# Attention of a two-block network: the order of its token tiles is reversed

## The chip, the cores and the metric

One NeuronCore of a Trainium2 chip runs the whole network as one program. The metric is the device time of one execution in microseconds (us). Engines are named as the profile names them: PE (TensorE), DVE (VectorE), ACT (ScalarE), POOL (GpSimd), SP (SyncE, which issues most DMAs).

## The reference, cut to what matters

The input is 512 tokens of width 1024, in float32. The first block has two layers; each is a feed-forward part, a hybrid mixer, and a second feed-forward part. The second block has two layers of another kind, which the change does not touch. In the mixer, one projection feeds three branches; only the attention branch and the projection matter here:

```python
proj = h @ w_in                                   # 512 x 1024 by 1024 x D_IN
# attention, 8 heads in 2 groups of 4, head width 64, blocks of 128 query tokens
p_s = masked_softmax(q @ k_sel.T + bias_s, dist_s >= 0)    # "selected": top_n covers all blocks
p_w = masked_softmax(q @ k_win.T + win_bias, causal mask)  # "window" of 512 = all tokens
o   = g0 * o_c + g1 * (p_s @ v_sel) + g2 * (p_w @ v_win)
```

With 512 tokens both attentions are causal attention over all earlier tokens: a query tile i (128 tokens) needs keys of tiles 0 to i, that is (i + 1) * 128 keys. The query tiles do not depend on each other. `masked_softmax` subtracts the row maximum, exponentiates and divides by the sum.

## The kernel before, in words

The program is a sequence of stages. A stage has one instruction stream for each engine, written out by hand, and ends with a barrier of all engines. Products of float32 values are made from a high part (`..._high`, rounded) and a low part (`..._low`, the rest), with three matmuls (`product`, lines 163 to 165). The high part is made by ACT (a CAST), the low part by DVE (`low_part`, line 170).

The change lies in `mixer1_attend`, the stage `attn_0` in the first layer and `attn_1` in the second. It does two things at once:

- **Attention.** `pairs` lists 16 steps p, each a query tile i and a head a of each group (so two heads). Every step has two half steps m = 2p + b: b = 0 for the selected keys, b = 1 for the window keys. For a half step, PE makes the scores (`scores(m)`, line 1430), DVE adds the bias and takes the row maximum (`biased(m)`, line 1576, and line 1580 for the shift), ACT exponentiates (`exps(m)`, line 1525), PE transposes the probabilities (`turn(m)`, line 1441), ACT and DVE copy the two groups out (`copy(m)`, lines 1533 and 1586), and PE multiplies with the values (`values(m)`, line 1455). After both half steps DVE combines (`combine(p)`, lines 1593 to 1606). The width of all this is `keys(m)` = (i + 1) * 128.
- **Dense pieces.** The part LATE of the projection (20 output tiles in 8 chunks of weights: 12 wide ones of 512 columns, 8 narrow ones of 256) is cut into pieces of 2 or 4 of the 8 contraction steps. `dense_plan` spreads these pieces, in a fixed order, over the 32 half steps, in proportion to `room` = 10.0 - 1.6 * (i + 1) of the half step. It counts 0.68 for a contraction step of a wide tile, 0.36 for a narrow one.

The PE order in one step p is: `scores(2p)`, `turn(2p-2)`, `dense(2p)`, `scores(2p+1)`, `values(2p-2)`, `turn(2p-1)`, `dense(2p+1)`, `values(2p-1)`. `scores(m)` waits until `biased(m-1)` is done, since all scores use the same two PSUM banks. A dense tile n waits until tile n-2, which used its bank, is evacuated.

In half step h, after their attention work, ACT and DVE evacuate the tiles that ended in half step h-1 and make the high and low parts of the next chunks of weights (`next_pieces`: four quarters for each of chunks 2 to 7). Chunk 0 is split at the head of the stage, one contraction step after another. Chunk 1 is split whole: `round_high(1)` stands in ACT's stream behind `exps(0)`, and `round_low(1)` in DVE's between `biased(0)` and `biased(1)`. DVE also has one convolution for each of the six `raw` tiles (`convolve`, lines 1623 to 1628), two half steps after the tile's last piece, and `positions` (line 1635). SP loads a chunk once the chunk two before it is split, and the next stage's first weights once the last chunk is split.

Of the kernel before, what the change touches and what calls it, by code (L numbers as in the profile page):

```python
# [24 lines left out]
TT = T // P  # L25
# [11 lines left out]
HPG = HEADS // GROUPS  # L37
# [1203 lines left out]
def mixer1_part(w_in, order):  # L1241
    chunks = mixer1_chunks(w_in)
    return [chunks[c] for c in order]
# [130 lines left out]
def mixer1_attend(nc, M, A, I, l, mine, ahead):  # L1374
# [2 lines left out]


    chunks, tiles = mixer1_part(I.w_in[l], LATE), mixer1_tiles(A, LATE)
    pairs = [(i, a) for i in range(TT) for a in range(HPG)]  # L1380
    N = len(pairs)
    plan = dense_plan(tiles, [10.0 - 1.6 * (i + 1) for i, _ in pairs for b in range(2)])
    half_of = {n: half for half, here in enumerate(plan) for n, _, end in here if end == DT}
# [902 lines left out]
def mixer1(nc, M, I, l, mine, ahead):  # L2286
    with ExitStack() as outer:
# [6 lines left out]
        with ExitStack() as memory:  # L2294
            sb = tensors(nc, memory, f"a{l}_")
            M.bias = sb("bias", HEADS, T)
            A.bias_all = M.bias
            A.qT = sb("qT", HPG, T)
            A.ksT, A.kwT = sb("ksT", T), sb("kwT", T)
            A.vs, A.vw = sb("vs", TT, KV), sb("vw", TT, KV)  # L2300
            A.gates = sb("gates", TT, HEADS * N_BRANCH)
            A.silz, A.dt, A.a = sb("silz", TT, D_SSM), sb("dt", TT, SH), sb("a", TT, SH)
            A.dt_e, A.dt_u, A.dt_r, A.dt_ln = (sb(f"dt_{x}", TT, SH) for x in "eurl")
            A.d_skip, A.norm_g = sb("d_skip", SG), sb("norm_g", SG)
            A.uv = sb("uv", TT, 2 * D_GMLP)
            A.raw = sb("raw", XT, T + SCONV - 1)
            A.blk = A.mix_local[:].rearrange("p i n -> p (i n)").rearrange("p (j m g n) -> p j m g n", j=2, g=GROUPS, m=PAIRS)
            A.zT = A.silz[:].rearrange("p i n -> p (i n)").rearrange("p (c t) -> p c t", t=T)
            A.gates_dtT = A.mix_local[0:HEADS * N_BRANCH + SH, 0, :]
            A.vT = A.mix[:, 0:2, :]  # L2310
            A.cmp_b = sb("cmp_b", CMP_HID)
            A.cmp_pos, A.cmp_w2, A.ws = sb("cmp_pos", 2, PAIRS), sb("cmp_w2", 2, 2, GROUPS, HD), sb("ws", GG, P)
            A.conv_w, A.conv_b, A.ws_b = sb("conv_w", SCONV, XT), sb("conv_b", XT), sb("ws_b", GG)
            A.ln_g, A.ln_b = sb("ln_g", D_GMLP), sb("ln_b", D_GMLP)
            A.dt_bias, A.a_log, A.a_neg = sb("dt_bias", SH), sb("a_log", SH), sb("a_neg", SH)
            rest_ahead = compression_ahead(nc, M, f"rest_{l}", I.cmp_w1[l])
            late_ahead = chunks_ahead(nc, M, f"attn_{l}", mixer1_part(I.w_in[l], LATE))
            late_ahead.landed.append(nc.alloc_semaphore(f"bias_landed_{l}"))
            mixer1_project(nc, M, A, I, l, mine, late_ahead, (l, 0))
            mixer1_attend(nc, M, A, I, l, late_ahead, rest_ahead)  # L2320
            mixer1_rest(nc, M, A, I, l, rest_ahead, rows_ahead)
# [755 lines left out]
```

## Time and profile before

| | us |
|---|---|
| median of 3 runs | 3687.22 (3684.85 to 3691.03) |
| the profiled execution | 3686.86 |
| its span in the profile | 3685.0 |
| stage `attn_0`, first matmul to the first of the next stage | 503.40 to 683.24 |
| stage `attn_1`, the same | 1606.19 to 1786.05 |

Times in the profile are from the start of the span. A matmul's row shows its whole passage, which overlaps the next one; consecutive starts tell the pace. In timelines, several like instructions are merged into one row (xcount), and brackets show how long the engine was idle before it and what released it.

### The profile page before, as it was taken

What the parts mean: (1) busy time and instruction counts of PE and PEld (TensorE: products, weight loads), DVE (VectorE), ACT (ScalarE), POOL (GpSimd) and SP (SyncE); (2) the same over time, 40 slices, a digit from 0 to 9 for tenths busy, and PEclk for the clock granted to TensorE, in tenths of its full rate; (3) what the DMA queues carried; (4) which work ended last, traced back from release to release, by engine and by line L of the source; (5) the groups of instructions that cost most, each with busy time, mean ns of one, the idle gap of its engine ahead of it and who ended that gap; (6) DMA issues with size and microseconds to landing.
All of it is one profiled execution on the core that took longest, in us unless ns stands there. A gap on an engine that the chain in (4) does not pass through costs nothing. (4 is left out here: it accounts for less than half of the span.)

```text
span 3685.0 us, 43312 instructions
## 1 busy us (share of the span) xinstructions
PE 3564.8 (97%) x17744; PEld 2935.6 (80%) x17744; DVE 1975.5 (54%) x3041; ACT 1226.1 (33%) x1928; POOL 149.2 (4%) x212
## 2 busy tenths in 40 slices
PE   6999999999999999999999999999999999999999
PEld 4888777678888888778678887788888878888887
DVE  5555566675456655566664355665322366553233
ACT  2222334532223222334532233635222355342222
POOL 1110100001000110100000001000000000000000
PEclk7999999999999999999999999999999999999999
DMA  6764241145443654331143342211333312113332
GB/s 237 228 200 128 74 114 47 52 142 195 143 137 97 212 176 127 81 107 47 52 132 116 107 138 53 71 45 52 90 93 124 100 48 75 41 52 103 98 103 80
DMA packets 438042, 397.74 MB, mean 108 GB/s; under 512 B 53780, under 2 KB 390276, under 8 KB 437845
## 3 DMA queue, kind: packets, MB, share of 16 engines
q1 hardware_dynamic: 413028, 310.53, 28.0%
q0 software_dynamic: 24816, 84.45, 6.7%
q8 instruction: 140, 2.29, 0.3%
q14 instruction: 58, 0.47, 0.0%
HBM read 390.14 MB, written 4.78 MB: 107 GB/s over the span
## 5 line engine op out<-in xcount | busy, mean ns | idle before, releaser
L163 PE MATMUL m_ps<-m_h_high,ffn_w_high 128*128 128x512 f32 x2100 | 822.4, 392 | 1.1 <-DVE ffn_w_low L170 1.1
L165 PE MATMUL m_ps<-m_h_high,ffn_w_low 128*128 128x512 f32 x2100 | 818.6, 390 | 0.0
L164 PE MATMUL m_ps<-m_h_low,ffn_w_high 128*128 128x512 f32 x2100 | 818.4, 390 | 0.0
L165 PEld LDWEIGHTS m_ps<-m_h_high,ffn_w_low 128*128 128x128 f32 x2100 | 395.0, 188 | 83.1
L163 PEld LDWEIGHTS m_ps<-m_h_high,ffn_w_high 128*128 128x128 f32 x2100 | 395.1, 188 | 82.9 <-issue 1.1
L164 PEld LDWEIGHTS m_ps<-m_h_low,ffn_w_high 128*128 128x128 f32 x2100 | 395.2, 188 | 81.3
L964 ACT ACTIVATE ffn_sil<-m_ps 128x512 f32<-128x512 f32 x132 | 79.0, 598 | 1131.2 <-PE m_ps L165 1131.2
L163 PE MATMUL m_ps<-ffn_w_high,ffn_hid_high 128*128 128x512 f32 x1056 | 412.2, 390 | 0.0
L165 PE MATMUL m_ps<-ffn_w_high,ffn_hid_low 128*128 128x512 f32 x1056 | 411.4, 390 | 0.0
L164 PE MATMUL m_ps<-ffn_w_low,ffn_hid_high 128*128 128x512 f32 x1056 | 411.3, 390 | 0.0
L1004 DVE TENSOR_TENSOR ffn_hid<-ffn_sil,m_ps 128x512 f32<-128x512 f32 x110 | 75.5, 687 | 549.0 <-ACT ffn_sil L964 549.0
L170 DVE TENSOR_TENSOR ffn_w_low<-m_raw,ffn_w_high 128x2048 fp32r<-128x2048 f32 (+1 forms) x168 | 303.7, 1823 | 111.9 <-ACT ffn_w_high L958 108.2
L170 DVE TENSOR_TENSOR ffn_w_low<-ffn_rows,ffn_w_high 128x1024 fp32r<-128x1024 f32 x132 | 161.6, 1224 | 291.8 <-ACT ffn_hid_high L972 291.7
L549 ACT CAST ffn_w_high<-ffn_rows 128x1024 fp32r<-128x1024 f32 x132 | 138.5, 1050 | 407.9 <-PE m_ps L165 391.6
L958 ACT CAST ffn_w_high<-m_raw 128x2048 fp32r<-128x2048 f32 x126 | 239.5, 1900 | 0.1
L165 PEld LDWEIGHTS m_ps<-ffn_w_high,ffn_hid_low 128*128 128x128 f32 x1056 | 198.5, 188 | 41.3
L163 PEld LDWEIGHTS m_ps<-ffn_w_high,ffn_hid_high 128*128 128x128 f32 x1056 | 198.7, 188 | 41.0
L164 PEld LDWEIGHTS m_ps<-ffn_w_low,ffn_hid_high 128*128 128x128 f32 x1056 | 198.6, 188 | 41.0
L387 DVE SCALAR_TENSOR_TENSOR ffn_ada_part<-ffn_rows,m_ccol,ffn_ada_part 128x512 f32<-128x512 f32 x224 | 168.2, 751 | 88.4 <-DMA ffn_rows<-in_ada_w 80.3
L163 PE MATMUL m_ps<-m_h_high,proj_w_high 128*128 128x512 f32 (+2 forms) x344 | 144.8, 421 | 8.5 <-DVE proj_w_low L170 8.4
L373 POOL DMA_DIRECT2D ffn_rows<-in_ada_w x128 | 90.9, 711 | 1500.8 <-issue 857.1
L164 PE MATMUL m_ps<-m_h_low,proj_w_high 128*128 128x512 f32 (+2 forms) x344 | 137.6, 400 | 0.0
(485 smaller groups left out, 5369.0 us busy)
## 6 DMA issues: line engine op xcount, KB each, us to landing
m_raw<-in_ffn_w SPq DMA_DIRECT2D x176, 512.0 KB, 4.8
ffn_rows<-in_ada_w POOLq DMA_DIRECT2D x128, 512.0 KB, 5.0
ffn_rows<-in_ffn_w SPq DMA_DIRECT2D x88, 512.0 KB, 3.4
m_raw<-in_w_in SPq DMA_DIRECT2D x32, 1024.0 KB, 5.7
m_raw<-in_ffn_w_gate SPq DMA_DIRECT2D x44, 512.0 KB, 3.7
m_raw<-in_ffn_w_up SPq DMA_DIRECT2D x44, 512.0 KB, 4.8
ffn_rows<-in_ffn_w_down SPq DMA_DIRECT2D x44, 512.0 KB, 3.7
m_raw<-in_w_out SPq DMA_DIRECT2D x24, 512.0 KB, 4.6
```

What stands on the lines that cost most here:

```text
L163: pe.matmul(out, sh, mh, start=first, stop=False, skip_group_check=True)
L164: pe.matmul(out, sh, ml, start=False, stop=False, skip_group_check=True)
L165: return pe.matmul(out, sl, mh, start=False, stop=last, skip_group_check=True)
L170: return dve.tensor_tensor(low, value, high.bitcast(F32), ALU.subtract)
L373: queue.dma_start(self.slots[:, n % 2], src).then_inc([S.ada0_landed, S.ada1_landed][n % 2], 16)
L387: dve.scalar_tensor_tensor(out=part, in0=self.slots[:, n % 2, j, :], scalar=self.M.ccol[:, k + j:k + j + 1], in1=part, op0=ALU.mult, op1=A ...
L549: return act.copy(self.high[f % self.SLOTS], self.raw[f % self.raws])
L958: act.copy(w_high[:, f % 2], M.raw[:, f % 2]).then_inc(S.wide_high, 1)
L964: act.activation(sil[:, f % 2, :], M.ps[:, 2 * (f % 2), :], ACT.Silu).then_inc(S.silu_done, 1)
L1004: dve.tensor_tensor(hid[:, f, :], sil[:, f % 2, :], M.ps[:, 2 * (f % 2) + 1, :], ALU.mult).then_inc(S.hidden_done, 1)
```

## The change

`pairs` lists the token tiles from the last (i = 3, 512 keys) to the first (i = 0, 128 keys). The heads keep their order. All else follows from `pairs`: the widths of each half step, the room, and the half steps in which dense pieces, evacuations, splits and convolutions fall.

```diff
     chunks, tiles = mixer1_part(I.w_in[l], LATE), mixer1_tiles(A, LATE)
-    pairs = [(i, a) for i in range(TT) for a in range(HPG)]
+    pairs = [(i, a) for i in reversed(range(TT)) for a in range(HPG)]
     N = len(pairs)
     plan = dense_plan(tiles, [10.0 - 1.6 * (i + 1) for i, _ in pairs for b in range(2)])
```

## Rows read from the trace of the kernel before

**Rows 1.** The page: its first line.
```profile
span 3685.0 us, 43312 instructions
```

**Rows 2.** Busy time by engine in both attention stages (PEclk: granted clock, 1 = full).
```profile
503.40:683.20 179.80, 174.16 (x1096) 139.96 (x1096) 117.05 (x389) 75.08 (x211) 0.00 (x0) 1.00 0.17 48
...
1606.20:1786.00 179.80, 174.19 (x1096) 139.95 (x1096) 117.11 (x389) 75.08 (x211) 0.00 (x0) 1.00 0.17 48
```

**Rows 3.** What PE waited for in `attn_0`: us in total, times, longest us.
```profile
PE m_ps L163 <- ACT a_uv L1268: 1.1, 1, 1.1
...
PE m_ps L163 <- DVE a_mix_local L1258: 0.9, 1, 0.9
...
PE m_ps L1455 <- ACT attn_turned L1533: 0.9, 5, 0.2
PE m_ps L163 <- DVE a_raw L1265: 0.6, 1, 0.6
PE m_ps L163 <- DVE attn_w_low L170: 0.4, 1, 0.4
```

**Rows 4.** Timelines of `attn_0`'s head: start us, us, engine, line, operation, [idle before].
```profile
503.40 0.49 PE L1430 MATMUL m_ps<-a_ksT,a_qT 64*128 64x128 f32 x4 [0.94 <-PEq L130]
...
508.57 0.49 PE L1430 MATMUL m_ps<-a_kwT,a_qT 64*128 64x128 f32 x4
...
513.29 0.49 PE L1430 MATMUL m_ps<-a_ksT,a_qT 64*128 64x128 f32 x4
...
506.50 0.28 DVE L1576 CUSTOM_DVE_ANT_0 attn_probs<-m_ps,a_bias 128x128 f32<-128x128 f32 x1
...
509.94 2.29 DVE L170 TENSOR_TENSOR attn_w_low<-m_raw,attn_w_high 128x2048 fp32r<-128x2048 f32 x1 [2.74 <-ACT attn_w_high L1114]
...
508.03 1.89 ACT L1114 CAST attn_w_high<-m_raw 128x2048 fp32r<-128x2048 f32 x1
```

**Rows 5.** Timeline of half steps with 512 keys (i = 3).
```profile
664.40 0.69 DVE L1576 CUSTOM_DVE_ANT_0 attn_probs<-m_ps,a_bias 128x512 f32<-128x512 f32 x1 [3.48 <-PE m_ps L1430]
...
665.95 0.72 ACT L1525 ACTIVATE attn_probs<-attn_probs,attn_shift 128x512 f32<-128x512 f32 x1 [6.11 <-DVE attn_shift L1580]
...
666.70 1.13 PE L1430 MATMUL m_ps<-a_kwT,a_qT 64*128 64x512 f32 x4
...
667.38 0.56 ACT L1533 COPY attn_turned<-m_ps 128x512 f32<-128x512 f32 x1
...
667.99 2.00 PE L1455 MATMUL m_ps<-a_vs,attn_turned 128*128 128x64 f32 x16 [0.16 <-ACT attn_turned L1533]
...
669.83 1.04 PE L1441 MATMUL m_ps<-m_ident,attn_probs 128*128 128x128 f32 x8
```

**Rows 6.** Timeline of a half step with 128 keys, and one bank wait.
```profile
518.21 0.49 PE L1430 MATMUL m_ps<-a_kwT,a_qT 64*128 64x128 f32 x4
518.63 0.66 PE L1455 MATMUL m_ps<-a_vs,attn_turned 128*128 128x64 f32 x4
519.12 0.39 PE L1441 MATMUL m_ps<-m_ident,attn_probs 128*128 128x128 f32 x2
...
520.28 0.24 ACT L1533 COPY attn_turned<-m_ps 128x128 f32<-128x128 f32 x1
...
621.84 0.36 ACT L1268 COPY a_uv<-m_ps 128x256 f32<-128x256 f32 x1
...
622.26 0.39 PE L163 MATMUL m_ps<-attn_w_high,m_h_high 128*128 128x256 f32 x1 [1.09 <-ACT a_uv L1268]
```

**Rows 7.** Timeline of DVE: start of a convolution, and what follows it.
```profile
520.59 0.49 DVE L1623 TENSOR_SCALAR a_silz<-a_raw,a_conv_w 128x512 f32<-128x512 f32 x1
...
523.35 0.68 DVE L1265 COPY a_raw<-m_ps 128x512 f32<-128x512 f32 x1
```

**Rows 8.** A wait of PE in an earlier stage; PE busy (x), PEclk after it.
```profile
466.36 0.67 PE L163 MATMUL m_ps<-m_h_high,proj_w_high 128*128 128x512 f32 x1 [2.51 <-DVE proj_w_low L170]
...
466.36:469.80 3.44, 3.44 (x8) 0.52 0.80 176
```

## The prediction

> **What bounds the kernel now.** I read the page first, then the busy time of each engine over the two attention stages, then PE's waits there, then the timelines at the places where the order bites. Each attention stage is 179.8 us long and PE is busy for 174.2 us of it, at full clock, while DVE has 117 and ACT 75 [rows 2]. So PE sets the time, and the change neither adds nor removes PE work: the same scores, transposes, value products and dense pieces are issued in another order. The time can only move by the time in which PE stands still (and by PE's clock). Inside the stage the waits that the order can alter are few [rows 3]: 1.1 and 0.9 and 0.6 us for a PSUM bank that ACT or DVE had not yet evacuated, 0.9 in five small waits for ACT's copy of the turned probabilities, 0.4 for the first low part at the head. That is the ceiling of any gain: 3.9 us a stage, 8 us in all. What the new order can lose has no such ceiling, so I follow PE's stream through it.
>
> **The plan, worked out from dense_plan.** Before, the even and odd half steps of i = 0 hold about three wide pieces each (4.08 by the plan's own count, 0.68 a contraction step), those of i = 3 about one (1.36). The trace agrees with the count: from scores(1) at 508.57 to scores(2) at 513.29 [rows 4] are 4.72 us, of which 0.42 is scores (518.21 to 518.63 [rows 6]) and 4.3 the three pieces. After the change half steps 0 to 7 (i = 3) hold 1, 1, 2, 1, 1, 1, 2, 1 pieces, and half steps 24 to 31 (i = 0) hold 3, 2, 3, 3, 3, 2, 3, 3 (those of narrow tiles being 1.44 each). So the title's claim holds. What it means is that PE starts the stage with its smallest stock of filler, against the longest softmax chain.
>
> **The head, the largest term.** Lengths for 512 keys [rows 5]: scores 1.05 (four matmuls in 1.13 with the last one's passage); DVE from biased to ACT's exponential 1.55 (664.40 to 665.95), of which the signal that frees the score banks comes after about 1.3; exponentials 1.43 (665.95 to 667.38); values 1.84 (667.99 to 669.83); transposes 0.9 (1.04 less the overlap). A wide piece of six matmuls is 1.37, or 0.23 each.
> - scores(0) starts at 503.40 as before and ends at 504.45; the piece of dense(0) ends at 505.8. DVE begins biased(0) at 506.50 as before [rows 4], since the low parts of chunk 0 stand ahead of it, and its signal comes at 507.8. scores(1) waits for that. PE stands still from 505.8 to 507.85: 2.0 us. Before, 4.08 of dense work covered this.
> - scores(1) and the piece of dense(1) take PE to 510.3. scores(2) needs biased(1), and that stands in DVE's stream behind round_low(1), which needs ACT's round_high(1), which stands behind exps(0). In the new order: exps(0) from 506.50 + 1.55 = 508.05 to 509.5; round_high 1.9 (508.03 to 509.94 [rows 4]) to 511.4; round_low 2.2 (2.29 less the overlap) to 513.6; biased(1) signals at 514.9. scores(2) starts at 515.0 in place of 513.29. PE stands still from 510.3 to 515.0: 4.7 us.
> - The 0.4 at the head goes, since the longer scores(0) covers it. Head: 2.05 + 4.7 - 0.4 = 6.35 us a stage.
> - Bounds: with the 128-key chain as in [rows 4] (biased(1) would then signal about 512.7) 4.1 would be left even so; with every following action 0.3 later than read, 7.5. I take 6.35, for it rests on rows of the same instructions.
>
> **Half steps 3 to 7.** PE catches its breath with one or two pieces a half step, while DVE gets its first extras. Walking on with the same lengths: conv 0 falls in half step 4, 2.76 us on DVE (520.59 to 523.35 [rows 7]), between biased(4) and biased(5). biased(5) then begins 1.5 us after its scores; values(2) waits 0.25 for ACT's copy and values(3), whose copy stands behind the late exps(5), 0.75. Later convolutions fall in half steps 8, 10, 13, 15 and 17, where two pieces and 384 or 256 keys leave PE 5 to 7 us between one score set and the next but one; I find no further wait there, and allow 0.5 for small ones (there are five such of 0.2 now). Sum 1.5; bounds 0.5 and 7 (below, as a rival).
>
> **The late half steps.** A wait for a bank appears now wherever tile n begins in the very half step in which tile n-2 is evacuated, with little ahead of it: three times, 2.6 us [rows 3]. By the plan, the new order has this in half steps 25, 26, 27, 28 and 29, for tiles 13, 14, 15, 17 and 18, because eight narrow tiles are crowded into them. The evacuation stands behind exps and copy in ACT's stream. It is over 2.64 us after the start of the half step's scores: 2.07 to ACT's copy (518.21 to 520.28), 0.15 for the copy's pace, and 0.42 from an evacuation's start to PE's first matmul (621.84 to 622.26) [rows 6]. PE gets to its dense pieces after 1.06 in an odd half step (scores, values, transposes, 518.21 to 519.12 and 0.15) and after about 0.6 in an even one (no values). With 1.44 for a narrow piece that precedes: tile 13 waits 2.64 - 2.5 = 0.15, tiles 14 and 17 2.64 - 2.04 = 0.6 each, tiles 15 and 18, with nothing ahead, 1.6 each. Sum 4.55. Bounds 2.5 (ACT free earlier by 0.4 at each) and 6.5 (DVE late with biased by as much).
>
> **What goes.** The three bank waits (1.1 + 0.9 + 0.6) and the five small ones (0.9): 3.5, nothing else being late at those places. **What is hidden.** The tail: its last three value products and two transposes shrink from i = 3 to i = 0, but that PE work is in the head now, so it is moved, not saved; its waits for copies have the same chain with shorter links. I take 0, and at most half a microsecond either way. DMA: SP's next-stage load is issued once the last chunk is split, half step 23 before, 28 now, with three half steps of dense work and the tail behind it; the stage's SP issues are never what PE waits for [rows 3], and I take 0, or 2 us if that load were late.
>
> **PE's clock.** After 2.51 us of standing still PE's granted clock averaged 0.52 (1.2 GHz, where 1.00 is 2.4) over 3.44 us, in which only 8 matmuls went [rows 8]; at the piece's pace of 0.23 they take 1.8, so 1.6 was lost. The 4.7 us at the head are longer than that wait, so I add one such fall a stage: 1.6, bounds 0 (it lies in idle time) and 3.3. A fall already after the 2.0 us wait would cost nothing: the 2.4 us of work behind it have 4.7 idle behind them.
>
> The Trainium skill (TensorE: Matmul & The Clock Gate, "HAM oscillation — how this bites in real kernels") describes kernels whose short bursts of matmuls between waits throw the clock back again and again. The trace here shows single falls only. By that rule the head would pay twice, and the sum would be up to 3 us more.
>
> **Sum.** A stage: 6.35 + 1.5 + 4.55 - 3.5 + 1.6 = 10.5. Two stages with equal rows [rows 2]: 21. The profiled execution took 3686.86, its span is 3685.0 [rows 1], and 1.9 lie around it; that is 0.36 under the median. 3686.9 + 21 = 3708.
>
> **The rivals.**
> - *DVE becomes the bound in the first half of the stage.* Five convolutions of 2.76 fall beside 512- and 384-key steps, on DVE behind combine and copies. If each pushes a biased past PE by half its length, 1.4, a stage loses 7 more, 14 in all: about 3722. For: values(3) already waits by my walk. Against: DVE has 63 us of slack a stage [rows 2]. Chance 0.15.
> - *The head is covered after all, so not slower.* This needs the chain through round_high(1) and round_low(1) to be off PE's path, with scores(2) by 510.5. Then the head's 6.35 and the clock's 1.6 go, and 2.55 a stage are left, 5 in all: 3692; with a late part at its lower bound 3688, within 0.2%. It decides at a head cost under about 2 us a stage. Against it is that 513.29 was the time of scores(2) with shorter links. Chance 0.06.
> - *A net gain*: head free and no new bank waits; it ends at 3686.9 - 2 x 3.5 = 3680, just under 0.2%. Chance 0.03.
> - *The clock does not fall, and the late waits are half of what I read*: 21 - 3.2 - 4.5 = 13, 3700. Chance 0.16.
>
> **How the numbers follow.** The forecast, 3702 to 3716, has 0.60. A measurement tells about 0.2% (7.4 us) from no change. The range 3696 to 3720 leaves out the covered head and the far part of the DVE case. Slower by over 0.2%: 0.60 + 0.16 + 0.15 less a little for a combination of low ends, 0.89; same 0.08; faster 0.03.
>
> **What would show it.** In the new trace: scores(1) of each stage preceded by about 2 us idle released by DVE's biased, scores(2) by 4 to 5, starting near 515 where it was 513.29; granted clock 0.50 soon after in both stages; bank waits released by a_uv's evacuation near the stage's end, two of them over 1 us; the stage some 190 us long. It is wrong if scores(2) starts without a wait, if PE's waits in the stage sum to no more than now, or if convolutions are what PE's waits are traced to.

## The result, and the profile after

The changed kernel takes 3707.27 us (median of 4 runs, 3702.76 to 3714.69), the kernel before 3686.76 beside it (3684.85 to 3691.03). The ratio is 1.0054, with a 95% interval of 1.004 to 1.0068: slower by 20.5 us. Forecast were 3708 and a range of 3696 to 3720.

The span of the profiled execution is 3704.1 us, 19.1 more than before [rows 1]. The starts of the stages show where it lies: `attn_0` runs from 501.55 to 690.35, 188.8 us (179.84 before), `attn_1` from 1614.44 to 1803.19, 188.75 (179.86). That is 17.85 of the 19.1. The two stages behind them (`rest_0`, `rest_1`) are 1.4 us longer each. All other stages together are 1.5 us shorter: what lies ahead of the first attention stage is 1.85 shorter, the rest a few tenths longer.

The view of busy time over `attn_0` after the change answers to [rows 2]: 12.2 us without PE (188.90 less 176.72) in place of 5.6, and a mean granted clock of 0.98.

```profile
501.50:690.40 188.90, 176.72 (x1097) 141.80 (x1097) 117.41 (x389) 75.32 (x212) 0.00 (x0) 0.98 0.16 45
```

PE's waits in the same stage after the change (us in total, times, longest us) answer to [rows 3]. The waits for `a_mix_local`, `a_raw` and `attn_w_low` are gone (the row with PEq is the wait at the barrier in front of the next stage); a new releaser, DVE's row maximum `attn_top`, leads.

```profile
PE m_ps L1430 <- DVE attn_top L1576: 6.1, 2, 4.4
PE m_ps L163 <- ACT a_uv L1268: 3.6, 4, 1.4
PE m_ps L1819 <- PEq L130: 1.4, 1, 1.4
PE m_ps L1455 <- ACT attn_turned L1533: 1.0, 3, 0.6
```

The head of the stage after the change, from the timelines of PE, DVE and ACT, answers to [rows 4]:

```profile
501.55 1.13 PE L1430 MATMUL m_ps<-a_ksT,a_qT 64*128 64x512 f32 x4 [0.94 <-PEq L130]
...
506.01 1.13 PE L1430 MATMUL m_ps<-a_kwT,a_qT 64*128 64x512 f32 x4 [1.74 <-DVE attn_top L1576]
...
513.11 2.08 PE L1430 MATMUL m_ps<-a_ksT,a_qT 64*128 64x512 f32 x4 [4.37 <-DVE attn_top L1576]
...
504.66 0.68 DVE L1576 CUSTOM_DVE_ANT_0 attn_probs<-m_ps,a_bias 128x512 f32<-128x512 f32 x1
...
509.54 2.29 DVE L170 TENSOR_TENSOR attn_w_low<-m_raw,attn_w_high 128x2048 fp32r<-128x2048 f32 x1 [3.38 <-ACT attn_w_high L1114]
511.75 0.68 DVE L1576 CUSTOM_DVE_ANT_0 attn_probs<-m_ps,a_bias 128x512 f32<-128x512 f32 x1
...
507.62 1.89 ACT L1114 CAST attn_w_high<-m_raw 128x2048 fp32r<-128x2048 f32 x1
```

Read it as a chain: biased(0) at 504.66, exponentials until ACT's cast at 507.62, the cast until DVE's low part at 509.54, that until biased(1) at 511.75, and PE's scores(2) at 513.11, 11.56 us after scores(0). Before, they came after 9.89 us, without a wait [rows 4]. The matmuls that follow take 2.08 where four took 1.13, since PE's clock is now half. Busy time (PE, PEld, DVE, ACT), granted clock and DMA by stretches after the change show how long:

```profile
510.00:512.00 2.00, 0.00 (x0) 0.00 (x0) 2.00 (x2) 0.00 (x0) 0.00 (x0) 1.00 0.00 0
512.00:514.00 2.00, 0.89 (x2) 0.50 (x4) 1.47 (x7) 0.71 (x2) 0.00 (x0) 0.56 0.49 100
514.00:516.00 2.00, 2.00 (x8) 0.89 (x5) 0.77 (x3) 0.81 (x4) 0.00 (x0) 0.50 1.26 283
516.00:518.00 2.00, 2.00 (x9) 1.81 (x8) 1.41 (x4) 1.22 (x3) 0.00 (x0) 0.50 0.64 142
518.00:520.00 2.00, 2.00 (x8) 1.53 (x8) 0.00 (x0) 0.99 (x5) 0.00 (x0) 0.73 0.00 0
```

All later waits of over 0.1 us in the stage, from PE's timeline after the change: three behind the first convolutions and the change to 384 keys, then the four bank waits of the crowded end, then the next stage's start.

```profile
532.51 2.00 PE L1455 MATMUL m_ps<-a_vs,attn_turned 128*128 128x64 f32 x16 [0.16 <-ACT attn_turned L1533]
...
537.34 2.00 PE L1455 MATMUL m_ps<-a_vw,attn_turned 128*128 128x64 f32 x16 [0.56 <-ACT attn_turned L1533]
...
589.68 1.55 PE L1455 MATMUL m_ps<-a_vs,attn_turned 128*128 128x64 f32 x12 [0.31 <-ACT attn_turned L1533]
...
652.36 0.36 PE L163 MATMUL m_ps<-attn_w_high,m_h_high 128*128 128x256 f32 x1 [0.44 <-ACT a_uv L1268]
...
658.03 0.39 PE L163 MATMUL m_ps<-attn_w_high,m_h_high 128*128 128x256 f32 x1 [1.33 <-ACT a_uv L1268]
...
665.58 0.39 PE L163 MATMUL m_ps<-attn_w_high,m_h_high 128*128 128x256 f32 x1 [0.35 <-ACT a_uv L1268]
...
671.37 0.47 PE L163 MATMUL m_ps<-m_h_high,attn_w_high 128*128 128x512 f32 x1 [1.43 <-ACT a_uv L1268]
...
690.35 0.36 PE L1819 MATMUL m_ps<-a_a,m_tri 128*128 128x16 f32 x2 [1.39 <-PEq L130]
```

### The profile page after: what moved, and what is told of

It is laid out like the page before. It is cut to its first block and busy times, and to the rows that moved or that the text cites. A ratio compares the mean times of both kernels' runs of the same rounds, so it can differ in the third digit from the quotient of the medians.

```text
span 3704.1 us, 43314 instructions
## 1 busy us (share of the span) xinstructions
PE 3570.7 (96%) x17744; PEld 2939.9 (79%) x17744; DVE 1976.2 (53%) x3041; ACT 1227.9 (33%) x1928; POOL 149.6 (4%) x212
## 5 line engine op out<-in xcount | busy, mean ns | idle before, releaser
L1525 ACT ACTIVATE attn_probs<-attn_probs,attn_shift 128x512 f32<-128x512 f32 (+3 forms) x128 | 71.1, 556 | 217.8 <-DVE attn_shift L1580 217.8
```

The costliest lines, as they stand in the source:

```text
L1525: ins = act.activation(probs(m, g), probs(m, g), ACT.Exp, bias=shift[:, m % 4, g:g + 1], accum_out=sums[:, p % 4, g, b:b + 1])
```

## The experiments

My theory (H) was that the loss is made at the head, by too little filler before biased(1), with the clock behind it, and to a smaller part late, by crowded narrow tiles. The rivals were the late part as the larger one (L), the long chain itself (O), and DVE (D). Ratios are to the kernel before, timed on the same chip. "Stage" is `attn_0` in the profiled execution, from its first scores to the next stage's first matmul.

| kernel | order of i | pieces in half steps 0, 1 | stage, us | median, us | ratio (95%) |
|---|---|---|---|---|---|
| before | 0 to 3 | 3, 3 | 179.8 | 3686.8 | 1 |
| changed | 3 to 0 | 1, 1 | 188.8 | 3707.3 | 1.0054 (1.004 to 1.0068) |
| e1, split later | 3 to 0 | 1, 1 | 189.0 | 3707.7 | 1.0053 (1.004 to 1.0065) |
| e2, room as before | 3 to 0 | 3, 3 | 176.4 | 3679.3 | 0.9978 (0.9968 to 0.9988) |
| e3, room reversed only | 0 to 3 | 1, 1 | 194.0 | 3719.1 | 1.0082 (1.0069 to 1.0094) |
| e4, waits overfilled | 3 to 0 | 1, 1 | 189.2 | 3708.0 | 1.006 (1.0047 to 1.0073) |
| e4b, waits filled | 3 to 0 | 1, 1 | 186.0 | 3702.9 | 1.0045 (1.0033 to 1.0058) |
| e5, evacuate first | 3 to 0 | 1, 1 | 184.4 | 3700.1 | 1.0034 (1.0021 to 1.0048) |
| e10, head filled | 3 to 0 | 3, 3 | 182.5 | 3697.8 | 1.0028 (1.0017 to 1.004) |
| e9, even room | 3 to 0 | 2, 2 | 178.9 | 3687.9 | 0.9998 (0.9989 to 1.0007) |
| e7, before, evacuate first | 0 to 3 | 3, 3 | 178.4 | 3687.1 | 1.0 (0.9991 to 1.0009) |
| e8, e2 and evacuate first | 3 to 0 | 3, 3 | 175.3 | 3682.1 | 0.9986 (0.9977 to 0.9995) |

**e2 and e3: the two halves of the change alone.** One line of code does two things: it reverses the tiles, and it reverses `room`. e2 keeps the new tiles and the old room, e3 the old tiles and the new room.

```diff
-    plan = dense_plan(tiles, [10.0 - 1.6 * (i + 1) for i, _ in pairs for b in range(2)])
+    plan = dense_plan(tiles, [10.0 - 1.6 * (TT - i) for i, _ in pairs for b in range(2)])
```

> The reversed token tiles, but the dense pieces spread as before the change (most of them in the first half steps, now those of 512 keys). Theory H, with the missing filler as the cause: scores(1) waits for nothing, scores(2) for about 1.2 us, no fall of the clock, the late bank waits are gone; stages of about 181 us, 3689 in all. Rival O (the order itself: the long chain of 512 keys first): the head's waits stay above 4 us a stage and the time above 3700. Rival D (DVE becomes the bound where convolutions meet 512-key steps): the head is free, but waits behind DVE of 5 us or more a stage appear in the first 12 half steps, 3697 or more.

> The token tiles in the old order (128 keys first), but the dense pieces spread as after the change (one piece in each of the first half steps). Theory H with the missing filler as the cause: scores(1) waits 1.8 us, scores(2) 3.8, then half clock; in the late half steps, now of 512 keys, the bank waits are 1.3 to 1.7 each and 6 in all; stages of about 191 us, 3709 in all. Rival O (the long chain first is the cause): head waits under 2 us a stage, and no more than 3695.

e2 is faster than the kernel before, by 0.22%. PE's waits in its stage, from the timeline of e2, are one at the head and two for banks:

```profile
514.69 1.13 PE L1430 MATMUL m_ps<-a_ksT,a_qT 64*128 64x512 f32 x4 [0.74 <-DVE attn_top L1576]
...
614.51 0.38 PE L163 MATMUL m_ps<-attn_w_high,m_h_high 128*128 128x256 f32 x1 [0.58 <-DVE a_mix_local L1258]
...
643.65 0.39 PE L163 MATMUL m_ps<-attn_w_high,m_h_high 128*128 128x256 f32 x1 [0.93 <-ACT a_uv L1268]
```

Six pieces ahead of scores(2) in place of two, and its wait is 0.74, without a fall of the clock in the stage. So O falls, and D too: the convolutions meet 512-key steps here, and PE waits for none of them. The stage is even 3.4 us shorter than before, where I had expected 1 us more. e3, with the short chain first, is the slowest kernel of all, which O did not allow either (it had at most 3695); its stage is 3 us longer than I had expected. Its timeline has the head's two waits, shorter than in the changed kernel as the 128-key chain is shorter, two longer waits for ACT's copies in the first quarter, where one piece is all that covers a convolution, and five bank waits near the end (5.5 us, where 6 were expected). The waits at the head and for the copies:

```profile
506.05 0.49 PE L1430 MATMUL m_ps<-a_kwT,a_qT 64*128 64x128 f32 x4 [1.11 <-DVE attn_top L1576]
...
511.70 0.80 PE L1430 MATMUL m_ps<-a_ksT,a_qT 64*128 64x128 f32 x4 [3.58 <-DVE attn_top L1576]
...
527.25 0.66 PE L1455 MATMUL m_ps<-a_vw,attn_turned 128*128 128x64 f32 x4 [1.37 <-ACT attn_turned L1533]
...
542.99 0.66 PE L1455 MATMUL m_ps<-a_vw,attn_turned 128*128 128x64 f32 x4 [1.92 <-ACT attn_turned L1533]
```

The reversed room costs 12.4 us a stage with the new tiles (188.8 - 176.4) and 14.2 with the old (194.0 - 179.8). The reversed tiles gain 3.4 (179.8 - 176.4) with the old room.

**e1: the split of chunk 1 moved behind biased(1).** The second wait at the head hangs on ACT's cast and DVE's low part, which nobody needs before half step 6.

```diff
-                    if p == 0 and b == 0:
+                    if p == 0 and b == 1:
                         W.round_high(act, S, 1)
...
-                    if p == 0 and b == 0:
+                    if p == 0 and b == 1:
                         W.round_low(dve, S, 1)
```

> The changed kernel, with chunk 1's split (round_high on ACT, round_low on DVE) moved one half step later, behind exps(1) and biased(1). Theory H (the loss is made at the head: two waits of PE for biased, 1.7 and 4.4 us, and the half clock that follows the second): the 4.4 us wait shrinks to under 0.7, PE's granted clock stays 1.00 behind it, each attention stage goes from 188.8 to about 181.5 us, the time from 3707 to about 3693. Rival L (the loss is made late, by the dense tiles crowded into the 128-key half steps): the head's waits only move by a half step, and the time stays above 3702.

I expected 3693 and a stage of 181.5; measured are 3707.7 and 189.0. The time did not move; the number is the one that I gave to rival L, but not for its reason. The wait in front of scores(2) is gone; half of it stands in front of scores(3), since DVE's low part is now ahead of biased(2), and PE had only the transposes and the two pieces of half step 2 to do meanwhile. 1.7 us of waits are saved over the stage, and the half clock lasts longer by more than that is worth. The timeline of e1, and its busy time with the granted clock:

```profile
515.79 1.94 PE L1430 MATMUL m_ps<-a_kwT,a_qT 64*128 64x512 f32 x4 [2.37 <-DVE attn_top L1576]
...
518.01 2.40 PE L1455 MATMUL m_ps<-a_vs,attn_turned 128*128 128x64 f32 x10 [0.28 <-ACT attn_turned L1533]
```
```profile
514.00:516.00 2.00, 0.21 (x2) 0.21 (x4) 1.93 (x9) 0.03 (x1) 0.00 (x0) 0.99 0.29 45
516.00:520.00 4.00, 3.72 (x14) 2.15 (x12) 2.01 (x6) 2.85 (x9) 0.00 (x0) 0.50 1.06 240
520.00:524.00 4.00, 4.00 (x18) 3.86 (x19) 0.57 (x1) 1.43 (x5) 0.00 (x0) 0.50 0.00 0
524.00:526.00 2.00, 2.00 (x7) 1.56 (x6) 1.42 (x6) 0.00 (x0) 0.00 (x0) 0.50 0.00 0
526.00:528.00 2.00, 2.00 (x18) 1.93 (x19) 0.00 (x0) 0.00 (x0) 0.00 (x0) 0.95 0.04 8
```

A wait of 2.4 us was followed by 10 us at half clock, the wait of 4.4 in the changed kernel by 7.

**e4 and e4b: the head's waits filled with idle matmuls.** PE's stream gets matmuls whose result nobody reads, behind dense(0) and dense(1). They leave the chain as it is and take the clock's fall away.

```diff
                 dense(2 * p)
+                if p == 0:
+                    keep_running(pe, M, 2, 6)      # e4b: 4
...
                 dense(2 * p + 1)
+                if p == 0:
+                    keep_running(pe, M, 2, 16)     # e4b: 10
```

> The changed kernel, with 6 idle-keeping matmuls of 256 columns behind dense(0) and 16 behind dense(1), so that PE is busy while it would wait at the head; results go to a bank not in use. Nothing is saved but the clock. If the half clock costs what the trace reads (2.5 to 3 us a stage at the head): granted clock 1.00 throughout the head, scores(2) at the same distance from the stage's start (11.6 us), stages of 186 in place of 188.8, and 3702 in all. Rival (the half clock is hidden by waits that come anyway): within 1 us of the changed kernel, 3706 to 3708.

> As e4, with 4 and 10 keep-running matmuls in place of 6 and 16: each took 0.44 us there, twice what I had reckoned, so that run overfilled the waits by 3.2 us a stage. Now they should just fill 1.7 and 4.4. If the half clock costs 2.5 to 3 us a stage: granted clock 1.00 at the head, scores(2) 11.6 us after scores(0) as in the changed kernel, stages of 186 us, 3701 to 3702. If it costs nothing: 188.8 and 3707.

e4 says little by its time alone: each of these matmuls took 0.44 us, and scores(2) came 14.8 us after scores(0), 3.2 too late. Its stage of 189.2 less these 3.2 is 186.0. e4b has the right size: 11.55 us, as in the changed kernel (timeline and busy time of e4b; the timeline counts each of these matmuls as two).

```profile
510.47 4.48 PE L176 MATMUL m_ps<-m_tri,m_ident 128*128 128x256 f32 x20
514.99 1.13 PE L1430 MATMUL m_ps<-a_ksT,a_qT 64*128 64x512 f32 x4
```
```profile
503.44:520.00 16.56, 16.50 (x74) 11.46 (x76) 10.35 (x29) 10.85 (x25) 0.00 (x0) 1.00 0.51 128
```

The stage is 186.0 us: with the same chain, the clock alone cost 2.8. (In that execution's second attention stage, 187.5 us, the clock fell once later on; the median of 3702.9 is 4.4 under the changed kernel's, but the two were not timed side by side, and the intervals of their ratios overlap.)

**e10 and e5: the head alone, the late part alone.**

```diff
# e10
-    plan = dense_plan(tiles, [10.0 - 1.6 * (i + 1) for i, _ in pairs for b in range(2)])
+    plan = dense_plan(tiles, [9.4 if p == 0 else 10.0 - 1.6 * (i + 1) for p, (i, _) in enumerate(pairs) for b in range(2)])
# e5, ACT's stream: evacuate taken out of dense(half) and put ahead of exps
                 for b in range(2):
+                    evacuate("act", act, 2 * p + b)
                     if p < N:
                         exps(2 * p + b)
```

> The changed kernel, with room for three dense pieces in each of the first two half steps (all later ones keep their small-to-large order). It touches the head alone. Theory H: scores(1) waits for nothing, scores(2) for 0.7 us as in e2, no fall of the clock; the late bank waits stay (3 to 4.5 us a stage). Stages of 180 to 182 us, 3690 to 3694: by this the head and its clock are two thirds or more of the difference between the changed kernel and e2 (12.4 us a stage). Rival L (the late crowding is the larger part): above 3698. Rival D: waits behind DVE of over 2 us in half steps 2 to 16.

> The changed kernel, with ACT's evacuations of dense tiles moved ahead of its exponentials in every half step. It touches the late bank waits alone (0.44, 1.33, 0.35 and 1.43 us a stage in the changed kernel). Theory H + late (both parts are real, and they add): those four waits go, the head is as before (1.7 and 4.4 and a half clock), stages of 185.3 in place of 188.8 us, 3700 in all. Rival (the late waits are only the place where PE catches up with ACT, and would turn up at the tail): stages above 188, 3706 or more.

PE's waits in e10's stage, leaving out the barriers and one of 0.35 for DVE:

```profile
PE m_ps L163 <- ACT a_uv L1268: 2.8, 4, 1.4
PE m_ps L1455 <- ACT attn_turned L1533: 2.5, 7, 0.6
PE m_ps L1430 <- DVE attn_top L1576: 0.7, 1, 0.7
```

With the head filled the stage loses 6.3 us (188.8 to 182.5); what is left in front of scores(2) is as in e2. That is somewhat less than I expected. Its time of 3697.8 fits neither side: H was given 3690 to 3694, L above 3698. As half steps 2 to 7 hold only 7 pieces (8 in the changed kernel, 17 in e2), waits for ACT's copies grew from 1.0 to 2.5 us. So filling the head alone is worth half of the 12.4 us and not two thirds. The waits and the clock at the head are two thirds in the changed kernel (5.4 more us of waits than in e2, and 2.8 of clock), but the pieces that remove them are then missing behind the head.

With the evacuations first the four late waits are gone and the stage is 4.4 shorter, 0.9 more than they made up. Not all of that is the late crowding: the same edit also gives 1.2 us on e2, where the narrow tiles are not crowded (e8, below). That leaves 3.2 for the crowding, and with the head's 6.3 some 3 of the 12.4 us for the thin half steps between. This last part is a remainder and not measured by a run of its own.

**e9: two pieces everywhere.**

```diff
+    plan = dense_plan(tiles, [6.0 for i, _ in pairs for b in range(2)])
```

> The reversed token tiles with the same room in every half step (two pieces in nearly all). A dose between the changed kernel (one piece in each of the first two half steps) and e2 (three). If a piece at the head is worth its own 1.37 us: 3.4 us of waits at the head in place of 6.1 and 0.7, one fall of the clock behind the second wait (2 to 3 us), and no bank wait later on, since the narrow tiles are no longer crowded; stages of 181 us, 3689 to 3691. If it is the small-to-large order over the whole stage that costs, and not the head: stages within 1 us of e2's 176.4, 3680.

The dose fits. The waits at the head (timeline of e9) sum to 3.40 for four pieces, between 6.11 for two pieces in all and 0.74 for six: 1.33 to 1.36 us a piece, where a piece takes 1.37:

```profile
504.30 1.13 PE L1430 MATMUL m_ps<-a_kwT,a_qT 64*128 64x512 f32 x4 [0.38 <-DVE attn_top L1576]
...
511.40 2.08 PE L1430 MATMUL m_ps<-a_ksT,a_qT 64*128 64x512 f32 x4 [3.02 <-DVE attn_top L1576]
```

There is no other wait in that stage. It is 178.9 us, 2 less than I expected. In part that is the fall of the clock, which was short this time (some 3.4 us). e2's stage explains the number: 176.4, and 2.7 more of waits at the head, less the 1.5 of bank waits that e9 does not have, and by my estimate 1.6 for 3.2 us of work at half clock, is 179.2.

**e7 and e8: the order of ACT's work, without and with the reversed tiles.** The edit of e5, on the kernel before and on e2.

> The kernel before, with ACT's evacuations ahead of its exponentials. One wait of PE behind ACT's evacuation is left there, 1.09 us a stage. Expected: it goes, stages of 178.7 in place of 179.85 us, 3685. With e2 and e8 this tells whether the reversed order gives anything that the order of ACT's work does not: if so e7 stays over 3 us above e8 in stage time (175.3).

> e2 (reversed token tiles, pieces spread as before the change) with ACT's evacuations ahead of its exponentials. Only one wait behind ACT is left in e2, 0.93 us a stage. Expected: it goes, stages of 175.5 in place of 176.4 us, 3677 to 3678, faster than the kernel before by 0.25%. If ACT's evacuations push the exponentials back: no change from e2 or worse.

In stage time both did what was expected (178.4 and 175.3), and the reversed tiles, with the old room, are worth 3.4 us a stage with the one order of ACT's work and 3.1 with the other. In total time neither shows it: e7 can't be told from the kernel before, and e8 is not better than e2 (3682.1 and 3679.3, on two chips). One microsecond a stage is below what these runs resolve. e2 and e8 both beat the kernel before.

## Why the prediction was right

The mechanism is the one forecast, but that the time is met within 1 us is luck: two misses cancel in it. Point by point:

- **What bounds.** PE, with its own work unchanged: all 17744 matmuls are there, and the waits and the clock account for the 9 us a stage (6.5 more of waits, 2.8 of clock). Held.
- **The head.** 2.0 and 4.7 us forecast, 1.74 and 4.37 measured, scores(2) 11.56 us after scores(0) where 11.6 was forecast. The chain was the one named. e9, e10 and e2 show that filler is what is missing.
- **Half steps 3 to 7 and on.** 0.25, 0.75 and 0.5 forecast; 0.16, 0.56 and 0.31 measured, the second at values(3) behind exps(5), as walked.
- **The late bank waits.** Forecast in half steps 25 to 29 as 0.15, 0.6, 1.6, 0.6 and 1.6; measured none, 0.44, 1.33, 0.35 and 1.43. Right places, all about 0.2 too long: 3.55 for 4.55. e5 shows the cause: with the evacuations ahead of the exponentials all four are gone.
- **What goes.** 3.5 forecast and gone. I had kept the tail at 0; its two waits of 0.4 went as well, and the next stage starts 0.5 later behind its barrier (1.39 for 0.91), a net gain of 0.36.
- **The clock.** Forecast 1.6 a stage, from one earlier fall; 2.8 by e4b. It stayed at half for about 7 us rather than 3.4, the first part in the wait. This term was mis-sized.
- **Outside the stage.** Attention gave 9.0 a stage and not 10.5. The missing 3 us were made good by what I had not forecast, and put at nothing: `rest_0` and `rest_1` were 1.4 longer each, with PE's waits in `rest_0` as before but for the barrier, and a granted clock of 0.56 and 0.59 at 710 to 714 (busy time after the change):

```profile
710.00:712.00 2.00, 1.65 (x4) 1.11 (x5) 0.92 (x2) 1.98 (x3) 0.00 (x0) 0.56 1.01 277
712.00:714.00 2.00, 2.00 (x15) 1.67 (x13) 0.52 (x4) 0.07 (x1) 0.00 (x0) 0.59 1.04 242
```

Whether the change caused this stays open. The same stage took 59.65 us in one layer of e2 and 61.1 in the other, so the reversed tiles don't always bring it. But it goes along with them: in the twelve profiled executions together, `rest_0` or `rest_1` took 61.0 us or more in 16 of 18 cases behind reversed tiles, and in 1 of 6 behind the old order (the other five took 59.65 to 59.75). No run tests why.

The rule that I weighed from the Trainium skill (TensorE: Matmul & The Clock Gate, "HAM oscillation — how this bites in real kernels"), that short bursts between waits throw the clock back again and again, is not what the trace shows here: there was one stretch at half clock in the stage's head each time, not several. The clock did cost more than the single fall that I had added, but because the stretch was twice as long as the earlier one; in e1, with waits of 1.7 and 2.4 us, it was 10 us.

What the prediction did not see is that the line held a gain as well. The reversed tiles alone gain 3.4 us a stage (e2 against before). 2.0 of them are waits: 3.6 us in e2's stage, the barrier at its end included, against 5.6. The other 1.4 lie in time that the profile counts as PE busy, and they are spread over many groups of matmuls, none with more than 0.4; waits shorter than a matmul's overlap with its predecessor would hide there, but no run here separates them, and it stays open.

## What to carry to other kernels

Before you reverse a loop, list everything that is derived from its order. Here one expression fed both the sequence of tiles and the share of filler per step; the first was worth 3.4 us a stage, the second cost 12.4, and separating them gave a kernel 0.22% faster than the one before. At the head of a software pipeline count the filler up to the first result that the bottleneck engine must wait for: give the most filler there and where a convolution or a cast stands in the way, whatever the average room is. And moving a wait is no gain while filler stays as scarce: e1 took 1.7 us of waits away and lost as much again to the clock.

## What the runs showed of the hardware that was not expected

- PE's half clock is not priced by the wait ahead of it. At the wait of 4.4 us the clock was at 0.50 for some 7 us (2.8 us lost, by e4b), at 3.0 us in e9 for some 3.4, and at 2.4 us behind an earlier 1.7 in e1 for 10. One and the same wait of 1.52 us in `rest_0` was followed by no fall in the kernel before and by 10 us at half clock in e9 (the wait in both timelines, then e9's busy time and granted clock):

```profile
703.22 0.44 PE L1842 MATMUL m_ps<-m_ident,rest_cmp_x 128*128 128x128 f32 x2 [1.52 <-ACT rest_cmp_x L1965]
...
698.72 0.44 PE L1842 MATMUL m_ps<-m_ident,rest_cmp_x 128*128 128x128 f32 x2 [1.52 <-ACT rest_cmp_x L1965]
...
700.70:708.70 8.00, 8.00 (x33) 5.92 (x33) 4.66 (x15) 0.41 (x1) 0.00 (x0) 0.50 0.87 204
```
- Filling a wait of PE with matmuls that nobody reads gave back the clock's share and nothing else: 2.8 us a stage.
- Single falls of the clock in other stages, at places that differ between executions of kernels with the same code there, move a stage by 1.4 us and more (`rest_0` and `rest_1` took 59.65 to 64.4 us), so changes of a microsecond a stage can be read in the trace of the stage and not in the total.
